# A third tile of quarter sums on GpSimd, and the last block's transposes in three groups

## The chip, the cores and the metric

The kernel runs on one core of a Trainium2 chip. The time is device microseconds of one execution; the number of a kernel is the median of its runs. Five engines run their own instruction queues, in order, and wait for each other on semaphores: PE (TensorE), DVE (VectorE), ACT (ScalarE), POOL (GpSimd) and SP (SyncE, which only issues DMAs here).

## The reference

One layer of a diffusion backbone over 1152 tokens of width 1024: 128 context tokens and 1024 latent ones. Two token mixers (a chunked bidirectional mLSTM and a pooling mixer) are merged and added to x; then comes the ConvFFN, at whose start the change lies:

```python
    y = jnp.einsum('bld,de->ble', jax.nn.sigmoid(ga) * ya + jax.nn.sigmoid(gb) * yb, w_out)
    x = x + gt1 * _rmsnorm(y, g_post_mix)
    h2 = _rmsnorm(x, g_pre_ffn) * (1 + sc2) + sh2
    up = _dwconv_rows(jnp.einsum('bld,df->blf', h2, w_up), conv_w, conv_b, grid)
    ug, uv = jnp.split(up, 2, axis=-1)
    f = jnp.einsum('blf,fd->bld', jax.nn.gelu(ug) * uv, w_down)
    x = x + gt2 * _rmsnorm(f, g_post_ffn)
```

`w_up` has 2 x 2816 columns: 22 blocks of 128 gate columns and 22 of value columns. The convolution has three taps along rows of 64 tokens.

## The kernel before

**Precision.** Every fp32 product is made of three passes over a high and a low part: x = hi + lo, and hi*hi, hi*lo, lo*hi are summed in PSUM. A split is two instructions: hi is a rounding copy (mostly ACT), lo is the difference (always DVE, recorded on L2375, the line of a helper).

**Tokens and features.** The 1152 tokens stand in three blocks b of 384, each of three tiles of 128. The normed input of the FFN, h2, is held with features on partitions: `H_hi` and `H_lo`, eight feature tiles k of 128 features by 1152 tokens. `w_out`'s product gives token tiles t = 0 to 8 with tokens on partitions, so h2 must be turned. Blocks 0 and 1 are turned through DRAM. The last block, b = 2, is turned by PE: `second_norm` (L1563) issues three transposes for a feature tile k into a PSUM bank, 6 or 7 in turn. From there `second_evac` on ACT (L2110, it calls `norm_evac`, L1802) writes scaled and shifted copies: `tsc2[k % 2]`, and for odd k `H_hi` too. On DVE `norm_split` (L2435) forms `H_hi` for even k and `H_lo` for all. `tsc2` has two slots, so the copy of turn k waits for the split of turn k - 2. `xt_free` counts evacuated turns, `h_split_done` the splits, 48 at the end of this stage.

**Where the turns stand.** PE's first products of the FFN are `first_up(half, b)` (L1698, half 0 gate and half 1 value), in the order (0,0), (0,1), (1,0), (1,1), (0,2), (1,2). Each is eight steps k of three matmuls with 384 columns (L1197 to L1199), into bank 3 * half + b. The table `LAST_TURNS` (L565) says behind which step a turn stands: turns 0 and 1 behind steps 6 and 7 of (1,0), turns 2 to 7 behind steps 0 to 5 of (1,1). (0,2) waits for the split of each k before its step k.

**Plain blocks.** The first three of the 22 feature blocks, f = 0, 1, 2, are done plainly: `plain_unit` on PE, and `plain_up(f, ...)` on ACT (L2180) and DVE (L2852). For each of three token blocks, first of the gate half and then of the value half, ACT writes the middle tap and the bias from PSUM (`conv_g`, `conv_v`, L2198), DVE adds the two outer taps (L2875, one input from PSUM), and for the gate ACT then applies gelu (L2203). `conv_gate_done` and `conv_value_done` count DVE's part. Weights come through a ring of three slots (`ring_hi` by ACT, `ring_lo` by DVE).

**Quarter sums.** The other 19 blocks are multiplied in a Strassen-like scheme, seven products instead of eight (`product(s, i, ...)`, L1591; its matmuls are on L1612). It needs sums of quarters of h2: `T1` to `T4`, each four feature tiles k by 576 tokens. `quarter_tiles(eng, done, k, before, lo, hi)` (L721) forms tile k of all four from `H_hi` and `H_lo`, in eight `tensor_tensor` instructions of 576 columns, lo to hi - 1 of them in one call; each waits for the one ahead of it. All are on L736. GpSimd does k = 0 and 1 (L1170), as soon as `h_split_done` is 48, and then `weight_sum(s, n)` for the weights (L1154). DVE does k = 2 and 3, in pieces that `between(f, block)` (L2973) puts behind the conv taps of a block (block is 0 to 2 for the gate half, 3 to 5 for the value half). `quarter_split(k)` rounds the four tiles on ACT (L2170, four instructions on L2177: `T_hi`) and takes the difference on DVE (L2845: `T_lo`). ACT's split of tile 2 stands ahead of `plain_up(2)`, its split of tile 3 between the halves of `plain_up(2)`.

**What the products wait for.** i = 0 and 1 use `H_hi` and `H_lo`; i = 0 waits for all nine gate blocks' taps (banks 0 and 1). i = 2 is the first that reads `T_hi` and `T_lo`: it waits for all four `quarter_lo`, the seventh value block's taps and its weight split:

```python
                if g == 0:
                    pe.wait_ge(conv_gate_done, NB * PLAIN)
                elif g == 2:
                    pe.wait_ge(conv_value_done, NB * (PLAIN - 1) + 1)
                pe.wait_ge(up_lo_done, g + 1)
                if s == 0:
                    pe.wait_ge(quarter_lo, KD // 2)
```

(`up_lo_done` is counted by `up_lo_split`, L2894; the last two lines stand in `up_pair`, ahead of i = 2.)

Of the kernel before, what the change touches and what calls it, by code (L numbers as in the profile page):

```python
# [30 lines left out]
KD = DM // P  # L31
# [4 lines left out]
NB = 3  # L36
# [72 lines left out]
def build(nc, x_prompt, x_sample, state_C, state_n, state_m, c, c_ctx, w_ada, b_ada, g_pre_mix, g_post_mix,  # L109
# [113 lines left out]
    def place(name, shape, dt=F32, at=None):  # L223
        size = int(np.prod(shape[1:])) * (2 if dt == BF16 else 4)
        off = base[0] if at is None else at
        if at is None:
            base[0] += (size + 31) // 32 * 32
        return nc.alloc_sbuf_tensor_at(name, shape, dt, offset=off)
# [117 lines left out]
    X1 = place("X1", [P, NT, DM], at=SC0 + 16 * T)  # L346
# [60 lines left out]
    ps = nc.alloc_psum_tensor("ps", [P, 8, 512], F32)  # L407
# [39 lines left out]
    xt_done, xt_free = S("xt_done"), S("xt_free")  # L447
# [38 lines left out]
    pool_sums, dve_sums = S("pool_sums"), S("dve_sums")  # L486
# [70 lines left out]
    def turned_block():  # L557

        return X1[:, 0:TB, :].rearrange("p t d -> p (t d)").rearrange("p (k s) -> p k s", s=BW)
# [2 lines left out]

        return z_turned[b].rearrange("(k p) s -> p k s", p=P)

    LAST_TURNS = {(1, 0): {6: 0, 7: 1}, (1, 1): {0: 2, 1: 3, 2: 4, 3: 5, 4: 6, 5: 7}}  # L565

    def out_bank(t):

# [152 lines left out]
    def quarter_tiles(eng, done, k, before, lo=0, hi=8):  # L721


        first, second = slice(0, HT), slice(HT, T)
        as_f32 = lambda ap: ap.bitcast(F32)
        x1, x2 = [[as_f32(h[:, k, c]) for h in (H_hi, H_lo)] for c in (first, second)]
        y1, y2 = [[as_f32(h[:, KD // 2 + k, c]) for h in (H_hi, H_lo)] for c in (first, second)]
        t1, t2, t3, t4 = [T_full[name][:, k, :] for name in quarters]
        steps = ((t1, x2[0], x2[1], ALU.add), (t2, y2[0], y2[1], ALU.add), (t3, t2, t1, ALU.subtract),
                 (t1, t1, x1[0], ALU.subtract), (t1, t1, x1[1], ALU.subtract), (t2, t2, t1, ALU.subtract),  # L730
                 (t4, y1[0], t2, ALU.subtract), (t4, t4, y1[1], ALU.add))
        for n, (out, a, b, op) in enumerate(steps):
            if lo <= n < hi:
                if n:
                    eng.wait_ge(done, before + n)
                eng.tensor_tensor(out, a, b, op).then_inc(done, 1)  # L736

    with nc.Block() as block:
# [288 lines left out]
        def _(pool):  # L1027
# [139 lines left out]
                pool.tensor_tensor(out, mid[f"g{half}"][:, :], mid[f"v{half}"][:, :], ALU.mult).then_inc(feature_done, 1)  # L1167

            pool.wait_ge(h_split_done, 2 * NB * KD)
            for k in range(2):  # L1170
                quarter_tiles(pool, pool_sums, k, 8 * k)
            for s in range(NP):
                weight_sum(s, 0)
# [15 lines left out]
        def _(pe):  # L1189
# [5 lines left out]
            def mm3(out, whi, wlo, xhi, xlo, first, last):  # L1195

                pe.matmul(out, whi, xhi, start=first, stop=False)  # L1197
                pe.matmul(out, whi, xlo, start=False, stop=False)  # L1198
                return pe.matmul(out, wlo, xhi, start=False, stop=last)  # L1199
# [36 lines left out]
            def norm_turn(Xt, out, b, k):  # L1236

                for j in range(TB):
                    mm = pe.transpose(out[:, j * P:(j + 1) * P], Xt[:, b * TB + j, k * P:(k + 1) * P], ident[:, :])
                return mm  # L1240
# [58 lines left out]
            for b in range(NB):  # L1299
# [5 lines left out]
                for k in range(KD):  # L1305
                    w = slice(k * P, (k + 1) * P)
# [213 lines left out]
            for d in range(KD):  # L1520
                s = S_YA + d
                pe.wait_ge(lo_ready, s + 1)
                for b in range(NB):
                    take0(3 * (U_YA + d) + b)
                    r = s % RS
                    for n, k in enumerate(HEAD_ORDER):
# [3 lines left out]
                        w = slice(k * P, (k + 1) * P)  # L1530
# [32 lines left out]
            def second_norm(b, k):  # L1563
                if k == 0:

                    pe.wait_ge(x_scaled, NT + TB * (b + 1))
                w = b * KD + k
                if k >= 2:
                    pe.wait_ge(xt_free, NB * KD + w - 1)
                norm_turn(X1, ps[:, 6 + w % 2, :], b, k).then_inc(xt_done, 1)  # L1570

            pe.wait_ge(evac1, 3 * KD)
            for t in range(NT):
# [124 lines left out]
            def first_up(half, b):  # L1698
                bank, done = ((0, done0), (3, done1))[half]
                r = (S_FF + half) % RS  # L1700
                if b == 0:
                    pe.wait_ge(lo_ready, S_FF + half + 1)

                    pe.wait_ge(evac2, NT) if half else pe.wait_ge(evac0, Q_FF)

                for k in range(KD):
                    if half == 0:
                        pe.wait_ge(h_split_done, KD * (NB + b) + k + 1)
                    w = slice(k * P, (k + 1) * P)
                    tok = slice(b * BW, (b + 1) * BW)  # L1710
                    mm = mm3(ps[:, bank + b, 0:BW], ring_hi[:, r, w], ring_lo[:, r, w], H_hi[:, k, tok],
                             H_lo[:, k, tok], k == 0, k == KD - 1)
                    if k in LAST_TURNS.get((half, b), ()):
                        second_norm(NB - 1, LAST_TURNS[half, b][k])
                mm.then_inc(done, 1)


# [17 lines left out]
        def _(act):  # L1735
# [66 lines left out]
            def norm_evac(src_of, ready, freed, coefA, sh, n0, tile, slots, b, ks=range(KD), direct=True):  # L1802

                for k in ks:
                    w = n0 + b * KD + k
                    ready(b * KD + k)
                    if w - n0 >= slots:

                        act.wait_ge(h_split_done, w - slots + 1)
                    parts = [(0, 0, P), (1, P, BW)] if b == 0 else [(1, 0, BW)]  # L1810
                    for cond, lo, hi in parts:
                        outs = [tile[:, w % slots, lo:hi]]
                        if direct and b and k % 2:

                            outs.append(H_hi[:, k, b * BW + lo:b * BW + hi])
                        for out in outs:
                            ins = act.activation(out, src_of(b * KD + k)[:, lo:hi], ACT.Identity,
                                                 scale=coefA[:, k, cond:cond + 1], bias=modT[:, sh + k, cond:cond + 1])
                    ins.then_inc(freed, 1)
# [253 lines left out]
            for d in range(KD):  # L2073
# [3 lines left out]
                k = HEAD_ORDER[d]  # L2077
                if k < HG:
                    w = load_of[("hm", k)]
                    act.wait_ge(tile_in[w % LS], 16 * (w // LS + 1))  # L2080
                else:
                    w = load_of[("o", k)]
# [27 lines left out]
            def second_evac(b, ks):  # L2110

                if b < NB - 1:
                    norm_evac(lambda w: turned_block()[:, w % KD, :], lambda w: act.wait_ge(turned_in, 48 if b else 16), xt_free,
                              coefA2, 24, 24, tsc2, 2, b, ks)
                else:
                    norm_evac(lambda w: ps[:, 6 + w % 2, :], lambda w: act.wait_ge(xt_done, NB * KD + w % KD + 1), xt_free,
                              coefA2, 24, 24, tsc2, 2, b, ks)

            for t in range(NT):
# [49 lines left out]

            def quarter_split(k):  # L2170

                if k >= 2:
                    act.wait_ge(dve_sums, 8 * (k - 1))
                else:
                    act.wait_ge(pool_sums, 8 * (k + 1))
                for name in ("T2", "T3", "T1", "T4"):
                    ins = act.activation(T_hi[name][:, k, :], T_full[name][:, k, :], ACT.Copy)  # L2177
                ins.then_inc(quarter_hi, 1)
# [186 lines left out]
        def _(dve):  # L2365
# [8 lines left out]
            def sub_hi(out, full, hi):  # L2374
                return dve.tensor_tensor(out, full, hi.bitcast(F32), ALU.subtract)  # L2375
# [394 lines left out]
            for d in range(KD):  # L2770
                if d == 4:
                    second_coef()
                k = HEAD_ORDER[d]
# [71 lines left out]
            def quarter_split(k):  # L2845

                dve.wait_ge(quarter_hi, k + 1)
                for name in quarters:
                    ins = sub_hi(T_lo[name][:, k, :], T_full[name][:, k, :], T_hi[name][:, k, :])
                ins.then_inc(quarter_lo, 1)  # L2850
# [122 lines left out]
            def between(f, block):  # L2973

                if (f, block) == (1, 1):
                    quarter_split(0)
                if (f, block) == (1, 2):
                    quarter_tiles(dve, dve_sums, 2, 0, 0, 3)
                if (f, block) == (1, 3):
                    quarter_tiles(dve, dve_sums, 2, 0, 3, 6)  # L2980
                if (f, block) == (1, 4):
                    quarter_tiles(dve, dve_sums, 2, 0, 6, 8)
                    quarter_tiles(dve, dve_sums, 3, 8, 0, 1)
                if (f, block) == (1, 5):
                    quarter_split(1)
                    next_weights(-1, 0)
                    next_weights(-1, 1)
                if (f, block) == (2, 0):
                    quarter_tiles(dve, dve_sums, 3, 8, 1, 5)
                if (f, block) == (2, 1):  # L2990
                    quarter_tiles(dve, dve_sums, 3, 8, 5, 8)
                if (f, block) == (2, 2):
                    quarter_split(2)
                if (f, block) == (2, 4):
                    quarter_split(3)
                    next_weights(-1, 2)

            plain_up(0, [[2], [3]])
# [159 lines left out]
```

## Time and profile before

| | |
|---|---|
| median of 3 runs | 1695.71 us (1695.4 to 1697.65) |
| the profiled execution, its own time | 1696.06 us |
| its span | 1694.2 us |
| mean granted clock of TensorE | 0.998 |
| busy: PE, DVE, ACT, POOL | 99%, 80%, 41%, 15% |

The span runs from the first to the last instruction. Busy time of PE is modelled from overlapping matmuls. Times in the views are microseconds from the start of the span. For reading them: a group such as "x4" is shown with the time from its first start to its last end, and an instruction that is held up by another engine after it has started shows that as a longer duration.

### The profile page before, as it was taken

The page shows a single profiled execution, that of the slowest core. Times are in us where ns is not written, and L with a number is a line of the kernel's source. Part 1 is how long each engine was busy: PE and PEld are TensorE (multiplying, and loading weights), DVE is VectorE, ACT ScalarE, POOL GpSimd, SP SyncE. Part 2 cuts the span into 40 slices and gives each one's busy share as a digit, 9 for nine tenths or more (in the row PEclk, how much of TensorE's full clock was granted, in tenths as well). Part 3 has the DMA queues.
Part 4 walks back from the last instruction along what each step waited for, and adds up shares of the span by engine and source line. Part 5 has one row for each costly group of instructions (what it writes and reads, how often), then busy time and mean ns, then how long its engine had stood idle before and what let it go on. Part 6 is the DMA issues. An engine that isn't in the chain of part 4 may idle for free.

```text
span 1694.2 us, 27385 instructions
## 1 busy us (share of the span) xinstructions
PE 1682.3 (99%) x10472; PEld 1602.8 (95%) x10472; DVE 1348.6 (80%) x2928; ACT 690.4 (41%) x1257; POOL 260.0 (15%) x260
## 2 busy tenths in 40 slices
PE   9999999999999999999999999999999999999998
PEld 4999999999999999999988999999999999888887
DVE  3789998899899887563655698888888788788998
ACT  4543222332333343641433644433434434444364
POOL 1010000000100100110010352444333333000000
PEclk9999999999999999999999999999999999999999
DMA  9314344464465653572367422323222221786876
GB/s 348 100 34 137 102 136 114 124 179 137 120 171 157 158 161 124 179 252 69 100 170 200 138 70 86 107 95 120 85 79 78 73 77 55 233 272 229 276 249 241
DMA packets 263494, 247.21 MB, mean 146 GB/s; under 512 B 55200, under 2 KB 207532, under 8 KB 263364
## 3 DMA queue, kind: packets, MB, share of 16 engines
q1 hardware_dynamic: 246516, 187.15, 37.3%
q0 software_dynamic: 11328, 40.36, 7.3%
q10 hardware_dynamic: 5520, 17.95, 2.7%
q8 instruction: 83, 1.36, 0.3%
q14 instruction: 47, 0.39, 0.1%
HBM read 186.99 MB, written 58.42 MB: 145 GB/s over the span
## 4 chain that ended last, share of the span: by engine, by line
PE 93%; DVE 3%; DMA 1%; SPq 1%; POOL 1%; ACT 1%; issue 0%; DVEq 0%; ACTq 0%
PE ps L1612 25%; PE ps L1197 12%; PE ps L1198 12%; PE ps L1199 12%; PE ps L1556 6%; PE ps L1630 5%; PE ps L1631 5%; PE ps L1629 5%; PE ps L1433 2%; PE ps L1435 2%; PE ps L1434 2%; DMA adaw<-in_w_ada_dram 1%; DVE T_full L736 1%; POOL T_full L736 1%; DVE T_lo L2375 1%; PE ps L1341 1%
## 5 line engine op out<-in xcount | busy, mean ns | idle before, releaser
L1197 PE MATMUL ps<-H_hi,ring_hi 128*128 128x384 f32 x1192 | 400.8, 336 | 0.1
L1199 PE MATMUL ps<-H_hi,ring_lo 128*128 128x384 f32 x1192 | 398.7, 334 | 0.0
L1198 PE MATMUL ps<-H_lo,ring_hi 128*128 128x384 f32 x1192 | 398.6, 334 | 0.0
L1197 PEld LDWEIGHTS ps<-H_hi,ring_hi 128*128 128x128 f32 x1192 | 223.9, 188 | 0.7 <-issue 0.6
L1198 PEld LDWEIGHTS ps<-H_lo,ring_hi 128*128 128x128 f32 x1192 | 223.9, 188 | 0.0
L1199 PEld LDWEIGHTS ps<-H_hi,ring_lo 128*128 128x128 f32 x1192 | 223.8, 188 | 0.0
L2375 DVE TENSOR_TENSOR up_lo<-up_raw,up_hi 128x512 fp32r<-128x512 f32 x114 | 88.4, 778 | 57.2 <-ACT up_hi L2168 57.2
L1612 PE MATMUL ps<-T_hi,up_hi 128*128 128x288 f32 x608 | 130.9, 297 | 2.1 <-DVE up_lo L2375 2.1
L1612 PE MATMUL ps<-T_hi,up_lo 128*128 128x288 f32 x608 | 131.0, 297 | 0.0
L1612 PE MATMUL ps<-T_lo,up_hi 128*128 128x288 f32 x608 | 130.7, 297 | 0.0
L2611 DVE SCALAR_TENSOR_TENSOR ada_part<-raw,condT,ada_part 128x128 f32<-128x128 f32 x448 | 120.4, 348 | 0.0
L1631 PE MATMUL ps<-B_hi,A_lo 128*128 128x512 f32 x308 | 119.9, 389 | 0.0
L1630 PE MATMUL ps<-B_lo,A_hi 128*128 128x512 f32 x308 | 119.9, 389 | 0.0
L1629 PE MATMUL ps<-B_hi,A_hi 128*128 128x512 f32 x308 | 119.9, 389 | 0.0
L1753 ACT ACTIVATE ring_hi<-raw 128x1024 fp32r<-128x1024 f32 (+1 forms) x61 | 60.9, 1000 | 128.5 <-DMA raw<-in_w_in_dram 61.8
L1612 PEld LDWEIGHTS ps<-T_hi,up_hi 128*128 128x128 f32 x608 | 98.6, 190 | 2.3 <-DVE T_lo L2375 2.3
L1612 PEld LDWEIGHTS ps<-T_hi,up_lo 128*128 128x128 f32 x608 | 98.7, 190 | 0.0
L1612 PEld LDWEIGHTS ps<-T_lo,up_hi 128*128 128x128 f32 x608 | 98.5, 190 | 0.0
L700 ACT ACTIVATE stage<-ps 128x384 f32<-128x384 f32 x72 | 35.1, 487 | 154.3 <-PE ps L1199 154.3
L1612 PE MATMUL ps<-H_hi,up_lo 128*128 128x288 f32 x456 | 97.9, 296 | 0.0
L1612 PE MATMUL ps<-H_hi,up_hi 128*128 128x288 f32 x456 | 97.8, 296 | 0.0
L2168 ACT ACTIVATE up_hi<-up_raw 128x512 fp32r<-128x512 f32 x114 | 68.9, 621 | 70.2 <-POOL up_raw L1154 70.0
(391 smaller groups left out, 3844.2 us busy)
## 6 DMA issues: line engine op xcount, KB each, us to landing
raw<-in_w_in_dram SPq DMA_DIRECT2D x44, 512.0 KB, 5.1
up_raw<-in_w_up_dram SPq DMA_DIRECT2D x38, 512.0 KB, 5.2
w_raw<-in_w_down_dram SPq DMA_DIRECT2D x66, 256.0 KB, 3.4
raw<-in_w_ada_dram SPq DMA_DIRECT2D x32, 512.0 KB, 5.5
X<-z_f SPq DMA_DIRECT2D x44, 256.0 KB, 3.9
GE<-z_gates SPq DMA_DIRECT2D x72, 128.0 KB, 4.0
w_sub<-in_w_down_dram SPq DMA_DIRECT2D x33, 256.0 KB, 3.9
adaw<-in_w_ada_dram SPq DMA_DIRECT2D x6, 1024.0 KB, 14.6
```

The source lines that it names most:

```text
L1197: pe.matmul(out, whi, xhi, start=first, stop=False)
L1198: pe.matmul(out, whi, xlo, start=False, stop=False)
L1199: return pe.matmul(out, wlo, xhi, start=False, stop=last)
L1556: mm = pe.matmul(ps[:, bank + hb, :], x[:, k, tok], w[:, hb * 512:(hb + 1) * 512], start=(n == 0 and first), stop=(n == KD - 1 and last))
L1612: mm = pe.matmul(ps[:, bank + sb, 0:SB], wt[:, w], x[:, k0 + k, cols], start=(k == 0 and n == 0), stop=(k == KD // 2 - 1 and n == 2))
L1629: pe.matmul(out, xhi, whi, start=first, stop=False)
L1630: pe.matmul(out, xhi, wlo, start=False, stop=False)
L1631: return pe.matmul(out, xlo, whi, start=False, stop=last)
L1753: act.activation(split_of(s)[0][:, 0:w], raw[:, n % RS, 0:w], ACT.Copy).then_inc(hi_ready, 2 if s == 1 else 1)
L2168: act.activation(up_hi[i][:, :], src, ACT.Copy).then_inc(up_hi_done, 1)
L2375: return dve.tensor_tensor(out, full, hi.bitcast(F32), ALU.subtract)
L2611: ins = dve.scalar_tensor_tensor(out=part, in0=w, scalar=condT[:, cond, k:k + 1], in1=part, op0=ALU.mult, op1=ALU.add)
```

## The change

Two parts. First, the turns of the last block: 0 to 3 stand together behind the last step of (1,0), 4 and 5 behind step 3 of (1,1), 6 and 7 behind step 1 of (0,2). They use banks 6, 7, 2, 5, 6, 7, 5, 6, so turn 4 waits for the evacuation of turn 0, 5 for 1, 6 for 3 and 7 for 4 (`TURN_AFTER`). (0,2) uses bank 2 and waits until turn 2 has been evacuated. Second, GpSimd forms the quarter sums of k = 2 too; DVE forms k = 3 alone, in four pairs of instructions, and its `T_lo` of k = 2 and 3 move one block earlier. The number of instructions of each kind is the same as before.

```diff
--- before.py
+++ after.py
@@ -562,7 +562,9 @@
 
         return z_turned[b].rearrange("(k p) s -> p k s", p=P)
 
-    LAST_TURNS = {(1, 0): {6: 0, 7: 1}, (1, 1): {0: 2, 1: 3, 2: 4, 3: 5, 4: 6, 5: 7}}
+    LAST_TURNS = {(1, 0): {7: (0, 1, 2, 3)}, (1, 1): {3: (4, 5)}, (0, 2): {1: (6, 7)}}
+    TURN_BANK = (6, 7, 2, 5, 6, 7, 5, 6)
+    TURN_AFTER = {4: 1, 5: 2, 6: 4, 7: 5}
 
     def out_bank(t):
 
@@ -1167,7 +1169,7 @@
                 pool.tensor_tensor(out, mid[f"g{half}"][:, :], mid[f"v{half}"][:, :], ALU.mult).then_inc(feature_done, 1)
 
             pool.wait_ge(h_split_done, 2 * NB * KD)
-            for k in range(2):
+            for k in range(3):
                 quarter_tiles(pool, pool_sums, k, 8 * k)
             for s in range(NP):
                 weight_sum(s, 0)
@@ -1564,10 +1566,9 @@
                 if k == 0:
 
                     pe.wait_ge(x_scaled, NT + TB * (b + 1))
-                w = b * KD + k
-                if k >= 2:
-                    pe.wait_ge(xt_free, NB * KD + w - 1)
-                norm_turn(X1, ps[:, 6 + w % 2, :], b, k).then_inc(xt_done, 1)
+                if k in TURN_AFTER:
+                    pe.wait_ge(xt_free, (NB + b) * KD + TURN_AFTER[k])
+                norm_turn(X1, ps[:, TURN_BANK[k], :], b, k).then_inc(xt_done, 1)
 
             pe.wait_ge(evac1, 3 * KD)
             for t in range(NT):
@@ -1703,6 +1704,8 @@
 
                     pe.wait_ge(evac2, NT) if half else pe.wait_ge(evac0, Q_FF)
 
+                if (half, b) == (0, NB - 1):
+                    pe.wait_ge(xt_free, (NB + b) * KD + 3)
                 for k in range(KD):
                     if half == 0:
                         pe.wait_ge(h_split_done, KD * (NB + b) + k + 1)
@@ -1711,7 +1714,8 @@
                     mm = mm3(ps[:, bank + b, 0:BW], ring_hi[:, r, w], ring_lo[:, r, w], H_hi[:, k, tok],
                              H_lo[:, k, tok], k == 0, k == KD - 1)
                     if k in LAST_TURNS.get((half, b), ()):
-                        second_norm(NB - 1, LAST_TURNS[half, b][k])
+                        for turn in LAST_TURNS[half, b][k]:
+                            second_norm(NB - 1, turn)
                 mm.then_inc(done, 1)
 
 
@@ -2113,7 +2117,7 @@
                     norm_evac(lambda w: turned_block()[:, w % KD, :], lambda w: act.wait_ge(turned_in, 48 if b else 16), xt_free,
                               coefA2, 24, 24, tsc2, 2, b, ks)
                 else:
-                    norm_evac(lambda w: ps[:, 6 + w % 2, :], lambda w: act.wait_ge(xt_done, NB * KD + w % KD + 1), xt_free,
+                    norm_evac(lambda w: ps[:, TURN_BANK[w % KD], :], lambda w: act.wait_ge(xt_done, NB * KD + w % KD + 1), xt_free,
                               coefA2, 24, 24, tsc2, 2, b, ks)
 
             for t in range(NT):
@@ -2169,8 +2173,8 @@
 
             def quarter_split(k):
 
-                if k >= 2:
-                    act.wait_ge(dve_sums, 8 * (k - 1))
+                if k == 3:
+                    act.wait_ge(dve_sums, 8)
                 else:
                     act.wait_ge(pool_sums, 8 * (k + 1))
                 for name in ("T2", "T3", "T1", "T4"):
@@ -2975,24 +2979,22 @@
                 if (f, block) == (1, 1):
                     quarter_split(0)
                 if (f, block) == (1, 2):
-                    quarter_tiles(dve, dve_sums, 2, 0, 0, 3)
+                    quarter_tiles(dve, dve_sums, 3, 0, 0, 2)
                 if (f, block) == (1, 3):
-                    quarter_tiles(dve, dve_sums, 2, 0, 3, 6)
+                    quarter_tiles(dve, dve_sums, 3, 0, 2, 4)
                 if (f, block) == (1, 4):
-                    quarter_tiles(dve, dve_sums, 2, 0, 6, 8)
-                    quarter_tiles(dve, dve_sums, 3, 8, 0, 1)
+                    quarter_tiles(dve, dve_sums, 3, 0, 4, 6)
                 if (f, block) == (1, 5):
                     quarter_split(1)
                     next_weights(-1, 0)
                     next_weights(-1, 1)
                 if (f, block) == (2, 0):
-                    quarter_tiles(dve, dve_sums, 3, 8, 1, 5)
+                    quarter_tiles(dve, dve_sums, 3, 0, 6, 8)
                 if (f, block) == (2, 1):
-                    quarter_tiles(dve, dve_sums, 3, 8, 5, 8)
-                if (f, block) == (2, 2):
                     quarter_split(2)
+                if (f, block) == (2, 3):
+                    quarter_split(3)
                 if (f, block) == (2, 4):
-                    quarter_split(3)
                     next_weights(-1, 2)
 
             plain_up(0, [[2], [3]])
```

## Rows read from the trace of the kernel before

**Rows 1.** Busy time of each engine, its share of the span, instructions.

```profile
PE 1682.3 (99%) x10472; PEld 1602.8 (95%) x10472; DVE 1348.6 (80%) x2928; ACT 690.4 (41%) x1257; POOL 260.0 (15%) x260
```

**Rows 2.** Waits of PE, 935 to 1060 us: total us, times, longest.

```profile
PE ps L1612 <- DVE up_lo L2375: 2.1, 1, 2.1
```

**Rows 3.** The chain that ended last: start us, us, what.

```profile
961.54 0.67 ACT H_hi L1817
962.24 0.57 DVE H_lo L2375
962.89 1.44 POOL T_full L736
...
1027.95 0.61 DVE up_lo L2375
```

**Rows 4.** Windows around the third L1612 product: PEclk is the granted clock.

```profile
1026.20:1030.00 3.80, 1.67 (x13) 1.47 (x12) 3.76 (x7) 1.66 (x4) 0.00 (x0) 1.00 0.00 0
1030.00:1033.50 3.50, 3.50 (x17) 3.50 (x17) 3.50 (x5) 0.00 (x0) 1.29 (x1) 0.51 0.46 181
```

**Rows 5.** PE's timeline, steps and turns of the last block: start us, us.

```profile
950.01 0.41 PE L1197 MATMUL ps<-H_hi,ring_hi 128*128 128x384 f32 x1
...
953.77 0.55 PE L1239 MATMUL ps<-ident,X 128*128 128x128 f32 x3
954.07 0.42 PE L1197 MATMUL ps<-H_hi,ring_hi 128*128 128x384 f32 x1
...
954.93 0.42 PE L1197 MATMUL ps<-H_hi,ring_hi 128*128 128x384 f32 x1
...
961.25 0.34 PE L1197 MATMUL ps<-H_hi,ring_hi 128*128 128x384 f32 x1
...
961.77 0.34 PE L1197 MATMUL ps<-H_hi,ring_hi 128*128 128x384 f32 x1
```

**Rows 6.** PE's timeline in the first stage, six transposes and what follows.

```profile
61.75 0.82 PE L1239 MATMUL ps<-ident,X 128*128 128x128 f32 x6
62.33 0.38 PE L1340 MATMUL ps<-vg_hi,H_hi 128*128 128x272 f32 x1
```

**Rows 7.** ACT's timeline; in brackets the idle time before, and its releaser.

```profile
954.36 0.67 ACT L1817 ACTIVATE tsc<-ps,modT,coefA 128x384 f32<-128x384 f32 x1 [1.63 <-PE ps L1239]
...
1003.36 2.41 ACT L2177 ACTIVATE T_hi<-T_full 128x576 fp32r<-128x576 f32 x4 [4.10 <-DVE T_full L736]
...
1019.61 2.40 ACT L2177 ACTIVATE T_hi<-T_full 128x576 fp32r<-128x576 f32 x4
```

**Rows 8.** DVE's timeline.

```profile
985.84 5.66 DVE L2375 TENSOR_TENSOR T_lo<-T_full,T_hi 128x576 fp32r<-128x576 f32 x4
...
998.17 1.74 DVE L736 TENSOR_TENSOR T_full<-T_full,H_lo 128x576 f32<-128x576 f32 x1
...
1008.95 1.51 DVE L2875 SCALAR_TENSOR_TENSOR conv_g<-ps,vT,conv_g 128x127 f32<-128x127 f32 x4
...
1019.06 2.75 DVE L2375 TENSOR_TENSOR T_lo<-T_full,T_hi 128x576 fp32r<-128x576 f32 x4
1022.59 2.68 DVE L2875 SCALAR_TENSOR_TENSOR conv_v<-ps,vT,conv_v 128x127 f32<-128x127 f32 x6 [0.78 <-ACT conv_v L2198]
```

**Rows 9.** The quarter sums by engine: durations min/median/max ns, first, last.

```profile
L736 POOL TENSOR_TENSOR T_full<-T_full x4: 1424/1432/1434, 966.8 to 985.0; 128x576 f32<-128x576 f32 x4
...
L736 DVE TENSOR_TENSOR T_full<-T_full x4: 749/758/758, 994.2 to 1015.6; 128x576 f32<-128x576 f32 x4
```

**Rows 10.** POOL's timeline: its last quarter sum, its second weight sum.

```profile
988.39 1.83 POOL L736 TENSOR_TENSOR T_full<-T_full,H_lo 128x576 f32<-128x576 f32 x1
...
997.56 1.73 POOL L1154 TENSOR_TENSOR up_raw<-up_raw 128x512 f32<-128x512 f32 x1
```

**Rows 11.** PE's timeline, the first and the third L1612 product.

```profile
1020.01 0.43 PE L1612 MATMUL ps<-H_hi,up_hi 128*128 128x288 f32 x2
...
1028.69 0.51 PE L1612 MATMUL ps<-T_hi,up_hi 128*128 128x288 f32 x2 [2.13 <-DVE up_lo L2375]
```

## The prediction

> **What bounds the kernel now.** The page first: PE is busy 99% of the span [rows 1], so nothing shortens the kernel but a wait of PE's, and over the span these are few. The view of waits, for PE from 935 to 1060 us, shows a single one of size: 2.1 us before a product of the feature halves (L1612), ended by DVE's up_lo [rows 2]. The chain of waits tells where it begins. It leaves PE at the last block's turns, goes through ACT and DVE to 962.8 us, through GpSimd's quarter sums from 962.89 on, and then through ACT and DVE to up_lo at 1028.6, after which PE runs on [rows 3]. So from 954 to 1029 us PE isn't the bound. The bound is the chain turns, splits, quarter sums, conv taps, T_lo, up_lo, and PE, which runs ahead of it, waits at its end.
>
> That wait costs twice. In the 3.8 us around it PE is busy for 1.67, and in the 3.5 us behind it the granted clock is 0.51, of full 2.4 GHz at 1.2, before it is 1.00 again [rows 4]. These 3.5 us at half clock lose (1 - 0.51) x 3.5 = 1.7 us. What the change can win here at most is therefore 2.1 + 1.7 us, and what PE saves at the turns.
>
> **The turns.** A step of three matmuls with no turn behind it takes 961.77 - 961.25 = 0.52 us, one with a turn 954.93 - 954.07 = 0.86, so a turn costs PE 0.34 [rows 5]. Does a group cost less? In the first stage six transposes stand together, and the next matmul begins 62.33 - 61.75 = 0.58 us after the first of them [rows 6]; two turns of 0.34 are 0.68, and the matmul behind a transpose is up to 0.1 late. So twelve transposes cost about four turns: I take 8 x 0.34 in both kernels. What PE saves is its waits between the turns. The first product of (1, 0) starts at 950.01 and (0, 2) at 961.77 [rows 5]; with sixteen steps and six turns and no wait it would start at 950.01 + 16 x 0.52 + 6 x 0.34 = 960.4, or 960.5 with a first step that is 0.1 longer. The last two turns, 0.7 us, then stand in (0, 2) itself, so PE is 0.6 us earlier at its end. Since PE runs ahead of the chain, that alone is worth nothing.
>
> The price is the chain's start. Turns 6 and 7 now come behind step 1 of (0, 2): 960.5 + 2 x 0.52 = 961.5. ACT sees a turn 954.36 - 953.77 = 0.6 us after its first transpose [rows 5, 7], so tsc of turn 6 starts at 962.1, and tsc and H_hi of turn 7 follow, each about 0.57 behind the last (0.67 long, a tenth of it overlapped), H_hi at 963.2. In the kernel before that H_hi starts at 961.54 [rows 3]: **+1.7 us** for the splits, for the quarter sums that wait for all 48 of them, and for every ring split behind. The first four turns don't make up for it, as turn 0 comes 0.5 us later than before too. The added wait for turn 2's bank in front of (0, 2) costs nothing: its evacuation is over by 957.5.
>
> **The quarter sums.** Tile 2's eight sums leave DVE. They take 0.76 us each and one of them 1.74 [rows 8, 9]: **-7.0 us**. But the sums of tile 3 and other work of DVE now run while GpSimd sums tile 2, and the two engines are in each other's way. A GpSimd sum takes 1.43, but 1.83 with DVE's T_lo beside it; the four T_lo of tile 0 take 5.66 us beside GpSimd and 2.75 alone, 2.9 more for some three meetings; a DVE sum that starts inside a GpSimd weight sum (997.56, 1.73 long) takes 1.74 for 0.76 [rows 8 to 10]. It looks as if the one waits until the other's instruction ends. I take 1.1 us for a meeting. (By the Trainium skill, GPSIMD Engine Reference, Key points, GpSimd shares its SBUF interfaces with VectorE and contends with instructions there that have two SBUF inputs or run in a 2-port mode. By this rule the conv taps, which read PSUM, stay as they are, and sums and splits pay, as in the trace. Its table of Engine selection says to keep elementwise work on VectorE as GpSimd is about twice slower; 1.43 against 0.75 agrees.)
>
> How many meetings are new? GpSimd's second tile ends at 988.39 + 1.83 = 990.2, the third begins 1.7 later and takes 8 x 1.5 plus 0.4 for each meeting, to some 1006.5, and two weight sums follow to 1010. DVE's two-input work in 992 to 1010 is the fourth T_lo of tile 0, ring_lo 5 and tile 3's first six sums, in pairs behind three blocks' taps. Of these eight I count six: a pair's first often falls in a gap. **+6.6 us.** ACT's work doesn't grow.
>
> **The order on DVE.** ACT does T_hi of tile 3 between the last gelu and the first conv_v of f = 2, 2.40 us from 1019.61, and DVE can't start conv_v's taps before 1022.59. In the kernel before DVE fills this gap with T_lo of tile 2, from 1019.06 for 2.75, and idles for 0.78 [rows 7, 8]. The change moves this T_lo ahead of the last gate block's taps, where it delays them, the gelu and T_hi, and leaves 1022.59 - 1019.1 = 3.5 us of idle time on DVE: **+2.7 us**. T_lo of tile 3, one block earlier than before, still ends before the same up_lo.
>
> **Sum.** up_lo, and PE's third product: +1.7 - 7.0 + 6.6 + 2.7 = +4.0 us, from 1028.7 to 1032.7 [rows 11]. A new wait of PE stands ahead of it: the first product needs the last gate block's taps, which ended at 1019.1 and now end at 1019.1 + 1.7 - 7.0 + 6.6 + 2.75 = 1023.1, while PE is there at 1020.0 - 0.6 [rows 8, 11]. The two products from 1020.01 to 1026.56 (1028.69 less 2.13) then take till 1029.7, or 1031.4 if the half clock falls on them: hidden before 1032.7. PE's second gap is thus 1.3 to 3 us instead of 2.1. Whether the clock falls again behind it, I can't read; if it doesn't, 1.7 us come back. I take half, -0.8: **+3.2 us**. The profiled execution took 1696.06, 1.9 more than its span and 0.35 more than the median of the runs, 1695.71; on that median the sum gives 1698.9.
>
> **Bounds.** If no meeting is new, 6.6 us go, and the path is PE's: third product at 1026.56 - 0.6 = 1025.9, -2.8, without a gap and so without half clock, -1.7: 1691.2. If each meeting costs a whole GpSimd instruction, 1.43, it is +2.0 and no clock comes back: +6.0, 1701.7. The turns' delay between 0 and 1.9, the gap on DVE between 2.0 and 2.75.
>
> **Rivals.**
> - Faster: sums on DVE and GpSimd hardly meet, or meet without cost, so that taking eight sums from DVE wins. For it: most of GpSimd's first tile ran at 1.43 beside DVE's taps. Against it: [rows 8, 10]. It decides below about 2.5 us for all new meetings. 1691.2.
> - Nothing measurable: the turns' delay is absorbed by the idle time that ACT and DVE have before 980 us, or fewer meetings, 3 of 6: +3.2 less 1.7 to 3.3, about 1697. Against it: the chain has no slack there.
> - GpSimd becomes the bound: ACT must wait for its third tile before the first conv_g of f = 2. Before, ACT waited 4.10 us for DVE's tile and began T_hi at 1003.36, and DVE came to those taps at 1008.95 [rows 7, 8], about 2.6 us after conv_g was written. Now T_hi begins at 1006.6, and DVE is there at about 1014 (1008.95 + 1.7 - 7.0 + 6.6, and five sums of tile 3, 3.8, that stood behind): some 4 us of margin. If GpSimd is later than that, each further us adds one: 1702 and more.
> - The change does nothing at the turns: grouping saves no time in PE. I hold this anyway; it is in the sum.
>
> **How the numbers follow.** The forecast has 0.60, faster 0.15, nothing measurable 0.17, GpSimd's bound 0.08. A measurement tells 0.2%, 3.4 us, from no change. The forecast of +3.2 lies beside this bound, with the clock's 0.8 to either side; I give 0.34 of its 0.60 to slower, 0.23 to the same and 0.03 to faster. Together: faster 0.18, the same 0.39, slower 0.43. The forecast's own range is 1696.5 to 1701.7; the range is 1692.3 to 1701.8, which leaves out the far end of the faster case and GpSimd's.
>
> **What would show it.** POOL's first T_full at 964.5 and not 962.9; turns 6 and 7 behind L1197's second step of (0, 2), and ACT's tsc after them; DVE's sums and T_lo near 1.8 where they meet GpSimd; a wait of PE of 3 to 4 us before the first L1612, ended by DVE's conv_g; DVE idle for 3.5 us until conv_v; the third product at 1032.7. I am wrong if PE enters L1612 without a wait, or if DVE's sums of tile 3 are all 0.76.

## The result, and the profile after

The kernel is slower: 1700.14 us, median of 14 runs (1699.14 to 1701.33), against 1695.64 for the kernel before on the same chip, also 14 runs. The ratio is 1.0026, with a 95% interval of 1.0019 to 1.0033: 3.2 to 5.6 us more. The profiled execution has a span of 1698.5 us. Line numbers of the changed kernel are up to four higher (L1612 is L1613, L2375 is L2379).

PE's line of the page hardly changes, and its waits, for the same stretch as in [rows 2], do:

```profile
PE 1684.3 (99%) x10472; PEld 1604.2 (94%) x10472; DVE 1348.8 (79%) x2920; ACT 690.1 (41%) x1257; POOL 276.0 (16%) x268
...
PE ps L1613 <- DVE conv_g L2879: 3.9, 1, 3.9
PE ps L1613 <- DVE up_lo L2379: 0.5, 1, 0.5
```

One wait of 2.1 us has become two, 4.4 in all, and the longer one stands ahead of the first product. The timeline of PE shows the groups of turns and both products:

```profile
953.72 1.47 PE L1241 MATMUL ps<-ident,X 128*128 128x128 f32 x12
954.95 0.42 PE L1199 MATMUL ps<-H_hi,ring_hi 128*128 128x384 f32 x1
...
960.94 0.81 PE L1241 MATMUL ps<-ident,X 128*128 128x128 f32 x6
...
1022.91 0.85 PE L1613 MATMUL ps<-H_hi,up_hi 128*128 128x288 f32 x2 [3.94 <-DVE conv_g L2879]
...
1032.40 0.50 PE L1613 MATMUL ps<-T_hi,up_hi 128*128 128x288 f32 x2 [0.46 <-DVE up_lo L2379]
```

The third product starts 3.7 us later than in [rows 11]. The windows around both products (span of time, sum, busy us and count of PE, PEld, DVE, ACT, POOL, then granted clock, DMA share, GB/s), to set against [rows 4], show half clock behind the first gap now, and none behind the third product:

```profile
1019.30:1023.00 3.70, 0.09 (x1) 0.09 (x1) 3.52 (x6) 0.95 (x3) 0.00 (x0) 0.79 0.00 0
1023.00:1027.00 4.00, 4.00 (x17) 4.00 (x18) 0.70 (x2) 4.00 (x8) 0.00 (x0) 0.50 0.37 150
...
1030.00:1033.50 3.50, 3.04 (x23) 2.83 (x22) 3.43 (x7) 1.68 (x3) 0.00 (x0) 1.00 0.00 0
...
1034.00:1038.00 4.00, 4.00 (x32) 4.00 (x31) 4.00 (x6) 0.00 (x0) 1.61 (x1) 1.00 0.55 193
```

At half clock the first two products take from 1022.91 to 1031.94 (1032.40 less 0.46), 9.0 us, where they took 6.55 before. That stretch hides almost whole in the wait for up_lo.

DVE's timeline, against [rows 8]:

```profile
986.89 6.89 DVE L2379 TENSOR_TENSOR T_lo<-T_full,T_hi 128x576 fp32r<-128x576 f32 x4
...
994.86 2.73 DVE L738 TENSOR_TENSOR T_full<-H_hi,H_lo 128x576 f32<-128x576 f32 x2
997.51 2.45 DVE L2379 TENSOR_TENSOR ring_lo<-raw,ring_hi 128x1024 fp32r<-128x1024 f32 x1
...
1002.09 1.87 DVE L738 TENSOR_TENSOR T_full<-T_full,H_hi 128x576 f32<-128x576 f32 x1
...
1005.90 1.87 DVE L738 TENSOR_TENSOR T_full<-T_full 128x576 f32<-128x576 f32 x1
...
1008.86 3.85 DVE L2379 TENSOR_TENSOR T_lo<-T_full,T_hi 128x576 fp32r<-128x576 f32 x4
...
1026.30 1.51 DVE L2879 SCALAR_TENSOR_TENSOR conv_v<-ps,vT,conv_v 128x127 f32<-128x127 f32 x4 [3.44 <-ACT conv_v L2202]
```

Four T_lo take 6.89 and 3.85 us where two groups at the same places took 5.66 and 2.75, sums take 1.87 where one alone takes 0.75, and DVE idles 3.44 us ahead of conv_v's taps, not 0.78. GpSimd's timeline beside it:

```profile
963.94 3.80 POOL L738 TENSOR_TENSOR T_full<-H_hi,H_lo 128x576 f32<-128x576 f32 x2 [11.63 <-DVE H_lo L2379]
...
997.05 1.83 POOL L738 TENSOR_TENSOR T_full<-T_full,H_hi 128x576 f32<-128x576 f32 x1
998.96 2.29 POOL L738 TENSOR_TENSOR T_full<-T_full,H_lo 128x576 f32<-128x576 f32 x1
...
1001.33 2.01 POOL L738 TENSOR_TENSOR T_full<-T_full 128x576 f32<-128x576 f32 x1
...
1005.33 1.82 POOL L738 TENSOR_TENSOR T_full<-T_full,H_lo 128x576 f32<-128x576 f32 x1
```

Read the two together. The DVE sum of 1002.09 ends at 1003.96, and the GpSimd sum that ran beside it at 1001.33 + 2.01 = 1003.34. The one of 1005.90 ends at 1007.77, its neighbour at 1007.15. ring_lo ends at 999.96, its neighbour at 998.88. Each DVE instruction ends 0.62 us (ring_lo 1.08, it has 1024 columns) behind the end of GpSimd's, whatever was left of that when it started: it stands still until GpSimd's instruction is over. It goes the other way too. GpSimd's next sum starts while DVE's is still on, and ends 1.29 us behind the end of that: at 1001.25 behind ring_lo's 999.96, at 1005.25 behind the sum's 1003.96. So when both have such work, they take turns.

### The profile page after: what moved, and what is told of

It reads as the page before. It is cut to its first block, busy times and chain, and to the rows that moved or that the text cites. A ratio compares the mean times of both kernels' runs of the same rounds, so it can differ in the third digit from the quotient of the medians.

```text
span 1698.5 us, 27386 instructions
## 1 busy us (share of the span) xinstructions
PE 1684.3 (99%) x10472; PEld 1604.2 (94%) x10472; DVE 1348.8 (79%) x2920; ACT 690.1 (41%) x1257; POOL 276.0 (16%) x268
## 4 chain that ended last, share of the span: by engine, by line
PE 84%; DVE 8%; DMA 3%; ACT 1%; POOL 1%; SPq 1%; issue 1%; DVEq 0%; ACTq 0%; POOLq 0%
PE ps L1613 18%; PE ps L1199 12%; PE ps L1200 12%; PE ps L1201 12%; PE ps L1558 6%; PE ps L1630 4%; PE ps L1632 4%; PE ps L1631 4%; PE ps L1435 2%; PE ps L1437 2%; PE ps L1436 2%; DVE mid_g L2929 1%; DVE up_lo L2379 1%; DMA w_sub<-z_w_diff 1%; DVE T_lo L2379 1%
## 5 line engine op out<-in xcount | busy, mean ns | idle before, releaser
L2379 DVE TENSOR_TENSOR up_lo<-up_raw,up_hi 128x512 fp32r<-128x512 f32 x114 | 89.7, 789 | 57.2 <-ACT up_hi L2172 57.2
L1613 PE MATMUL ps<-T_hi,up_hi 128*128 128x288 f32 x608 | 130.6, 296 | 1.0 <-ACT held_g L2214 0.6
L1613 PE MATMUL ps<-T_lo,up_hi 128*128 128x288 f32 x608 | 130.2, 296 | 0.0
L1613 PE MATMUL ps<-T_hi,up_lo 128*128 128x288 f32 x608 | 130.2, 296 | 0.0
L1613 PE MATMUL ps<-H_hi,up_hi 128*128 128x288 f32 x456 | 99.0, 299 | 3.9 <-DVE conv_g L2879 3.9
L1613 PEld LDWEIGHTS ps<-T_hi,up_hi 128*128 128x128 f32 x608 | 97.9, 189 | 1.9 <-ACT held_g L2214 1.1
L1613 PE MATMUL ps<-H_hi,up_lo 128*128 128x288 f32 x456 | 98.6, 298 | 0.0
L1613 PE MATMUL ps<-H_lo,up_hi 128*128 128x288 f32 x456 | 98.4, 298 | 0.0
L1613 PEld LDWEIGHTS ps<-T_hi,up_lo 128*128 128x128 f32 x608 | 98.0, 189 | 0.0
L1613 PEld LDWEIGHTS ps<-T_lo,up_hi 128*128 128x128 f32 x608 | 98.0, 189 | 0.0
```

Of the source, the lines that this page charges most:

```text
L1613: mm = pe.matmul(ps[:, bank + sb, 0:SB], wt[:, w], x[:, k0 + k, cols], start=(k == 0 and n == 0), stop=(k == KD // 2 - 1 and n == 2))
```

## The experiments

All differences below are against runs of the kernel before on the same chip, and their 95% intervals reach some 1.5 us to either side; what is finer than that is read from the traces, one of each kernel. The stages ahead of the FFN end up to 0.7 us apart from execution to execution, so times within a trace are counted from the first product of f = 0, at 941.38 us in the kernel before, 941.21 in the changed one, and between 941.00 and 941.70 in the others.

| kernel | time against before, us | first product of f = 0 to first T_full on POOL | first T_full to third product | first product of f = 0 to down stage |
|---|---|---|---|---|
| before | 0 | 21.51 | 65.80 | 507.72 |
| changed | +4.5 | 22.73 | 68.46 | 511.55 |
| turns_only | +1.5 | 22.73 | 65.78 | 508.90 |
| sums_only | +3.3 | 21.14 | 68.47 | 510.03 |
| splits_back | +3.1 | 22.73 | 67.04 | 509.32 |
| no_third_tile | -2.1 | 22.91 | 62.55 | 505.67 |
| filled_gap | +0.4 | 21.21 | 65.82 | 507.71 |
| reordered | -3.9 | 21.21 | 63.54 | 503.57 |
| reordered_turns | -2.9 | 22.73 | 62.63 | 504.66 |

**turns_only and sums_only: the change in two halves.** The first has the new `LAST_TURNS`, `TURN_BANK` and `TURN_AFTER` alone, the second all but these.

```diff
-    LAST_TURNS = {(1, 0): {6: 0, 7: 1}, (1, 1): {0: 2, 1: 3, 2: 4, 3: 5, 4: 6, 5: 7}}
+    LAST_TURNS = {(1, 0): {7: (0, 1, 2, 3)}, (1, 1): {3: (4, 5)}, (0, 2): {1: (6, 7)}}
+    TURN_BANK = (6, 7, 2, 5, 6, 7, 5, 6)
```

> The kernel before with the changed turns alone (groups of four, two and two, their banks and waits); the quarter sums as before. Theory (the chain from the last turn to up_lo has no slack): POOL's first T_full starts about 1 us later than in the kernel before (962.89), the third product about 1.7 later than 1028.69 less the shift of the origin, so near 1030.0, and the time is 1.2 to 1.7 above the kernel before, ratio 1.0007 to 1.0010. Rival 1 (the later turns are absorbed by idle time of ACT and DVE before 980 us): third product within 0.4 of 1028.7, time within 0.4. Rival 2 (what PE saves at the turns counts): 0.5 below.

> The kernel before with GpSimd's third quarter tile and the order on DVE and ACT that goes with it; turns as before. Theory (meetings of DVE and GpSimd at 1.1 us each, and the gap that ACT's T_hi of tile 3 leaves on DVE): third product near 1031.0 (+2.3), first product waits near 3 us for DVE's conv_g, time 2.3 to 3 above the kernel before, ratio 1.0014 to 1.0018, and this one's and turns_only's differences add up to the whole change's 4.5. Rival (meetings are free and the turns are all of the loss): at or below the kernel before, down to 1691.

Measured: turns_only 1697.56 us against 1696.04, ratio 1.0011 (1.0003 to 1.002); sums_only 1699.31, 1.0020 (1.0012 to 1.0029). Together 4.8, for 4.5 of the whole. At the start of the down stage the traces have +1.2 and +2.3; the profiled execution of sums_only has its remaining microsecond in the down stage, which takes 240.7 us there and 239.2 before, and why is open. Up to the third product the table parts the halves cleanly. The turns move the start of the quarter sums and nothing behind it (65.78 for 65.80). The sums leave the start alone and stretch what follows by 2.7. PE's saving at the turns is no gain anywhere: in turns_only PE waits longer, twice, for the same DVE results.

```profile
1020.35 0.53 PE L1613 MATMUL ps<-H_hi,up_hi 128*128 128x288 f32 x2 [1.26 <-DVE conv_g L2879]
...
1029.84 0.50 PE L1613 MATMUL ps<-T_hi,up_hi 128*128 128x288 f32 x2 [2.85 <-DVE up_lo L2379]
```

**splits_back: only the order on DVE undone.**

```diff
-                if (f, block) == (2, 1):
+                if (f, block) == (2, 2):
                     quarter_split(2)
-                if (f, block) == (2, 3):
+                if (f, block) == (2, 4):
                     quarter_split(3)
```

> The changed kernel with T_lo of tile 2 back behind the last gate taps of f = 2 and T_lo of tile 3 back behind the fifth block, as in the kernel before. Theory (moving T_lo ahead of the last gate taps cost 2.7 us, as DVE then stands idle while ACT does T_hi of tile 3): DVE's idle time ahead of conv_v near 1026 falls from 3.44 to under 1 us, the third product comes 2.7 earlier than 1032.40, near 1029.7, and the time falls from 1700.1 to about 1697.4. Rival (the end is set elsewhere, by GpSimd's third tile or by PE): the time stays within 0.7 of 1700.1.

Measured: 1699.17 us, 1.0019 (1.001 to 1.0028), 3.1 above the kernel before, where the changed kernel is 4.5 above it; in the trace the third product comes 1.4 us earlier, not 2.7. (The down stage comes 2.2 earlier; where the 0.8 between comes from is open.) The timelines, two lines of ACT and then DVE, show where the other 1.3 stay:

```profile
1019.56 0.52 ACT L2207 ACTIVATE conv_g<-conv_g 128x384 f32<-128x384 f32 x1 [2.60 <-DVE conv_g L2879]
1019.99 0.65 ACT L2202 ACTIVATE conv_g<-ps,vT 128x384 f32<-128x384 f32 x1
...
1020.68 1.26 DVE L2879 SCALAR_TENSOR_TENSOR conv_g<-ps,vT,conv_g 128x378 f32<-128x378 f32 x2 [1.15 <-ACT conv_g L2202]
1021.85 2.76 DVE L2379 TENSOR_TENSOR T_lo<-T_full,T_hi 128x576 fp32r<-128x576 f32 x4
1025.38 2.67 DVE L2879 SCALAR_TENSOR_TENSOR conv_v<-ps,vT,conv_v 128x127 f32<-128x127 f32 x6 [0.77 <-ACT conv_v L2202]
```

The gap ahead of conv_v closes, as expected (0.77). But a new one of 1.15 us opens ahead of the third gate block's taps: ACT can only start conv_g there (1019.99) after its gelu of the block before (1019.56), and with tile 2's sums gone nothing stands on DVE meanwhile; in the kernel before three sums of tile 3 stood there, 2.3 us. In the changed kernel T_lo of tile 2 fills that gap and leaves the other.

**no_third_tile: the same instructions on DVE and ACT, no third tile on GpSimd.** The splits of tile 2 read a tile of `H_hi`, so this kernel leaves out the sums of tile 2.

```diff
-            for k in range(3):
+            for k in range(2):
                 quarter_tiles(pool, pool_sums, k, 8 * k)
...
+                    src = H_hi[:, 2, 0:HT].bitcast(F32) if k == 2 else T_full[name][:, k, :]
-                    ins = act.activation(T_hi[name][:, k, :], T_full[name][:, k, :], ACT.Copy)
+                    ins = act.activation(T_hi[name][:, k, :], src, ACT.Copy)
```

> The changed kernel, with GpSimd's third quarter tile left out: the splits of tile 2 read a tile of H_hi in place of the sums, so that all of ACT's and DVE's instructions stay. Theory (six meetings at 1.1 us come from the third tile): DVE's T_full and T_lo from 992 to 1011 us fall to 0.75 each, the DVE chain is some 6.6 us shorter, PE is held by its own work, the third product at 1026 to 1027 and the time 1.5 to 3 below the kernel before, near 1693. Rival (long T_full and T_lo come from something else than GpSimd's instructions beside them): third product near 1032, time near 1700.

Measured: 1693.96 us, 0.9989 (0.998 to 0.9998). DVE's timeline, for the instructions shown above of the changed kernel:

```profile
987.19 5.64 DVE L2380 TENSOR_TENSOR T_lo<-T_full,T_hi 128x576 fp32r<-128x576 f32 x4
...
993.91 1.54 DVE L738 TENSOR_TENSOR T_full<-H_hi,H_lo 128x576 f32<-128x576 f32 x2
995.54 1.23 DVE L2380 TENSOR_TENSOR ring_lo<-raw,ring_hi 128x1024 fp32r<-128x1024 f32 x1
...
998.88 1.74 DVE L738 TENSOR_TENSOR T_full<-T_full,H_hi 128x576 f32<-128x576 f32 x1
...
1002.49 0.76 DVE L738 TENSOR_TENSOR T_full<-T_full 128x576 f32<-128x576 f32 x1
...
1004.33 2.76 DVE L2380 TENSOR_TENSOR T_lo<-T_full,T_hi 128x576 fp32r<-128x576 f32 x4
```

The third tile costs 1.25 us at the first T_lo group, 1.19 at the pair of sums, 1.22 at ring_lo, 1.11 at the sum of 1002.49, 1.09 at the second T_lo group and 0.2 at two others together: 6.1 us. From POOL's first sum to the taps of conv_v it is 56.46 us here (964.23 to 1020.69) and 62.36 in the changed kernel, 5.9 less. The sum of 998.88 takes 1.74 here too: it meets a weight sum (L1156), as the one of 998.17 did in [rows 8]. That meeting went over to another sum when tile 2's left DVE. The third product comes as much earlier, 5.9 (62.55 for 68.46). PE's own pace does not hold it, as the expectation had it: PE still waits 1.1 us for up_lo there.

**filled_gap: the kernel before, without its half clock.**

```diff
                 if s == 0:
+                    for _ in range(14):
+                        pe.matmul(ps[:, SLOT_BANK[2], 0:SB], H_hi[:, 0, 0:P], H_hi[:, 0, 0:SB], start=True, stop=True)
                     pe.wait_ge(quarter_lo, KD // 2)
```

> The kernel before, with 14 matmuls of 128x288 more in PE's gap ahead of the third product; their results are overwritten. They take some 1.9 us of the 2.1 us wait, so that PE is not idle there. Theory (through the up stage the chain over DVE sets the pace, not PE; runs so far show 420.2 to 420.4 us from the third product to the down stage whether the half clock falls behind that product or ahead of it): the granted clock behind the third product is 1.00 or the dip is shorter, the seventh product of the first pair starts up to 1.5 us earlier than 14.4 us behind the third, and the time does not change, within 0.4 of the kernel before. Rival (PE sets the pace, and the dip costs 1.7 us): the time falls by 1.3 to 1.7 us, ratio 0.9990 to 0.9992.

Measured: 1696.42 us against 1696.01, ratio 1.0001 (0.9993 to 1.001). The windows of [rows 4]:

```profile
1026.20:1030.00 3.80, 3.52 (x27) 3.32 (x27) 3.77 (x7) 1.15 (x3) 0.00 (x0) 1.00 0.00 0
1030.00:1033.50 3.50, 3.50 (x28) 3.50 (x28) 3.50 (x5) 0.00 (x0) 1.30 (x1) 1.00 0.55 207
```

The clock stays at 1.00, and the seventh product of the first pair starts at 1041.03, 12.9 us behind the third and not 14.4. But the down stage starts 507.71 us behind the first product of f = 0, for 507.72: the 1.5 us are gone. The loss can be followed from pair to pair. Counted from the first product of f = 0, the third product of the second pair comes 1.8 us earlier than in the kernel before (1.5 of the clock, 0.3 of a pause ahead of (1, 0) that only the trace of the kernel before has), that of the ninth at the same time (267.92 and 267.93). The reason is the pace of the two engines: in the kernel before, PE's third products of the second to the ninth pair follow each other every 22.4 us (1052.65 to 1209.31, seven pairs), but DVE's last held_g sums of a pair every 23.2 us from 1069.72 to 1185.97 (five pairs), and every 22.2 from 1208.13 on. A PE that is ahead comes to wait for DVE's results before that. PE now waits where it did not before: twice for ACT's held_g, 0.4 and 0.3 us, at 1169.68 and 1192.90, and up to 0.2 at several products around them. held_g in turn comes when DVE is done with the taps before it, at the same time in both kernels. The timelines of ACT, first of filled_gap, then of the kernel before:

```profile
1168.98 0.65 ACT L2212 ACTIVATE held_g<-ps 128x576 f32<-128x576 f32 x1 [3.49 <-DVE mid_g L2927]
```

```profile
1168.94 0.65 ACT L2210 ACTIVATE held_g<-ps 128x576 f32<-128x576 f32 x1 [3.47 <-DVE mid_g L2925]
```

**reordered and reordered_turns: another order, with the old division.** The kernel before, two tiles on GpSimd and two on DVE, with DVE's items behind its blocks of taps in this order (a block's number counts gate 0 to 2, value 3 to 5), and on ACT T_hi of tile 1 ahead of its last conv_v of f = 1.

```diff
+                if (f, block) == (0, 2):
+                    quarter_tiles(dve, dve_sums, 2, 0, 0, 1)
+                if (f, block) == (0, 4):
+                    quarter_tiles(dve, dve_sums, 2, 0, 1, 2)
+                if (f, block) == (1, 0):
+                    quarter_tiles(dve, dve_sums, 2, 0, 2, 3)
                 if (f, block) == (1, 1):
-                    quarter_split(0)
+                    quarter_tiles(dve, dve_sums, 2, 0, 3, 5)
                 if (f, block) == (1, 2):
-                    quarter_tiles(dve, dve_sums, 2, 0, 0, 3)
+                    quarter_split(0)
...
                 if (f, block) == (2, 2):
+                    quarter_tiles(dve, dve_sums, 3, 8, 7, 8)
+                    next_weights(-1, 1)
                     quarter_split(2)
-                if (f, block) == (2, 4):
                     quarter_split(3)
```

> The kernel before, its division of the sums (two tiles each) and its turns kept, but with DVE's work in another order: the first five sums of tile 2 one by one in the gaps in which DVE waits for ACT, from the end of f = 0 on; T_lo of tile 0 one block later, when GpSimd's second tile has ended; ACT's T_hi of tile 1 ahead of its last conv_v of f = 1; T_lo of tiles 2 and 3 both behind the last gate taps; up_lo 1 and 2 later. Theory (what counts is how often DVE's two-input work meets GpSimd's and how long DVE waits for ACT): T_lo of tile 0 takes about 2.8 us instead of 5.66, the DVE chain ends 3 to 4 us earlier, the third product comes at PE's own pace, 26.4 to 27.2 us behind 1000 for 1028.7 before, with a wait under 0.7 us, and the time is 1.5 to 2.3 below the kernel before. Rival (early sums only move the meetings, and delay the ring splits): third product within 0.5 of 1028.7, time the same.

> The same order on DVE and ACT, with the changed turns in groups. Theory (the turns delay the chain's start by 1.2 and save PE 0.6): where the chain now has slack at its end, the delay is partly hidden; third product between 0.6 earlier and 0.9 later than with the turns one by one, time within 0.7 of that run. Rival (the chain is still the bound everywhere): 1.2 to 1.5 later, as in the kernel with the turns alone.

Measured: reordered 1692.13 us against 1696.01, ratio 0.9977 (0.9968 to 0.9987), faster than both kernels; reordered_turns 1693.15, 0.9985 (0.9976 to 0.9994), 1.0 behind it. With the turns in groups the third product comes 0.6 us later (85.36 for 84.76 from the first product of f = 0), as expected, and the down stage 1.1; the time lies between the expected 0.7 and the rival's 1.2. In reordered PE has no wait in 935 to 1260 us. DVE's timeline:

```profile
990.77 2.83 DVE L2376 TENSOR_TENSOR T_lo<-T_full,T_hi 128x576 fp32r<-128x576 f32 x4
...
1013.88 6.54 DVE L2376 TENSOR_TENSOR T_lo<-T_full,T_hi 128x576 fp32r<-128x576 f32 x8
1020.34 3.83 DVE L2876 SCALAR_TENSOR_TENSOR conv_v<-ps,vT,conv_v 128x127 f32<-128x127 f32 x8
1024.09 1.28 DVE L2376 TENSOR_TENSOR up_lo<-up_raw,up_hi 128x512 fp32r<-128x512 f32 x2
...
1029.40 1.60 DVE L2912 TENSOR_TENSOR held_g<-held_g,ps 128x576 f32<-128x576 f32 x2
```

T_lo of tile 0 takes 2.83 us instead of 5.66, and eight T_lo stand in the gap that ACT's T_hi of tile 3 leaves, so that DVE goes on without an idle moment to its first held_g sums. Its first held_g sum starts 67.1 us behind POOL's first T_full, and 71.4 in the kernel before (1034.33): the chain is 4.3 us shorter. The third product gains 2.6 us, counted from the first product of f = 0, as PE has no wait left there. The down stage starts 4.15 earlier, and the other 1.6 are the half clock: without a wait the granted clock is 1.00 in each of five windows from 1018 to 1038 us, and the seventh product comes 12.8 us behind the third, not 14.4. Here the gain stays, since DVE is 4.6 us earlier than in the kernel before and PE never waits for it. The expectation of 1.5 to 2.3 left the clock out. These are several moves at once; how the gain on DVE divides among them no run shows.

## Why the prediction was right

The forecast was +3.2 us and 1698.9; measured were +4.5 and 1700.14, inside the range, by the mechanism that was forecast. That the sum met the third product within 0.1 us is in part luck: the terms are off by up to 0.9, and their errors cancel. The 1.3 us by which the change missed (+4.5 for +3.2) are the clock's term, 0.8, and some 0.5 in the down stage. (The chances do not add up to the last digit either: 0.17 + 0.23 is 0.40 and 0.34 + 0.08 is 0.42, where 0.39 and 0.43 stand.)

**The turns, +1.7.** POOL's first T_full came at 963.94, 22.73 behind the first product of f = 0, for 21.51 before and 21.1 to 21.2 in the three other kernels with turns one by one. Before's own trace has a pause of 0.3 us ahead of (1, 0) that these lack. So the turns cost 1.2 against that trace and 1.5 to 1.6 otherwise; turns_only measured +1.5 us. All of it reached the end. PE's own saving is the forecast 0.6: it is ready for the first product of the quarter scheme at 77.76, and at 78.36 in filled_gap. It was worth nothing, as written.

**DVE's sums, -7.0.** Mis-sized by 0.9. I took off the 1.74 of one of the eight sums, but its meeting with the weight sum stayed and only fell on another sum: 8 x 0.76 is 6.1.

**Six meetings, +6.6.** The five of size cost 1.1 to 1.25 each and two small ones 0.2: 6.1 us, by no_third_tile. The price of 1.1 held, the count was one too many.

**The order on DVE, +2.7.** The idle time came out as predicted (3.44). Putting the order back gives 1.4 only, as 1.15 us stay as the wait for ACT's gelu ahead of the third gate block, which now has nothing on DVE to hide it. I had not seen that wait: it comes from taking the sums away, not from the place of T_lo. The two are 2.6 together, for the +2.7.

**Their total.** -6.1 + 6.1 + 2.7 is +2.7 for the sums, where my terms gave +2.3; the traces show 68.46 - 65.80 = 2.66. With the turns it is 3.9 us at the third product (91.19 against 87.31 from the first product of f = 0), and the sum said +4.0. The first product's wait was predicted as 3 to 4 us, ended by conv_g, and is 3.94. The second gap was predicted as 1.3 to 3 us and is 0.46: the half clock cost the two products ahead of it 2.5 us (9.0 for 6.55), not 1.7. DVE's whole busy time, 1348.6 us before and 1348.8 after, says the same as the two equal terms.

**The clock, -0.8.** This term is wrong; it should be nothing. The half clock did stay away behind the third product (it fell behind the first), so PE ran the pair 1.5 us faster, but filled_gap shows that the kernel gains nothing by that. The changed kernel's own trace has it too: against the kernel before its third product is 3.9 us late in the first pair, 2.4 in the second and 3.8 from the ninth on. Through the first pairs of the up stage, to 1193 us, DVE sets the pace, and a PE that is ahead waits for it. [Rows 3] end where PE runs on, and I let the chain of DVE end there too. Without the term the forecast is 1699.7 on the median of 1695.71; the changed kernel measured 4.5 above the kernel before, +4.0 by that sum. The half microsecond left over lies in the down stage, which takes between 239.2 and 240.7 us (first to last matmul) in these traces with no order that follows the edits; its cause is open.

**The rivals.** Meetings that cost nothing: refuted by no_third_tile, which is what that case would have been, and it is faster than the kernel before. Slack ahead of 980 us: none, by turns_only. GpSimd the bound: ACT began conv_g at 1009.50 and DVE came to its taps at 1013.84, with conv_g written at 1010.15: 3.7 us of margin, for the 4 I had read. Grouping does save PE time, 0.6 us, but no run shows it at the end.

## What to carry to other kernels

Moving work from a busy engine to an idle one is worth what it takes off, less one meeting for each two-input instruction that the other engine now runs beside; here eight sums of 0.76 us were bought with 6.1 us of such meetings, and nothing was won. Look first for an order: of two kernels with the same instructions on each engine, the one whose T_lo stands behind GpSimd's last sum and whose long item fills DVE's wait for ACT is 3.9 us faster, 1.6 of them as PE's clock no longer falls. And when PE's wait disappears, ask whether the engine that it waited for is still late in the next stage before counting PE's gain.

## What the runs showed that was not expected

A half clock can be free, and it is so only while another engine is behind. Fourteen matmuls in a gap of 2.1 us kept the granted clock at 1.00 where it had been 0.51 for 3.5 us, and the time moved by +0.4 us within an interval of -1.2 to +1.7. In reordered, where DVE is 4.6 us earlier, the same full clock gives 1.6 us in the trace, and they stay.

A meeting costs what is left of the other's instruction. DVE's ends a fixed 0.62 us behind GpSimd's: the sum of 1005.04, beside a GpSimd sum that is over at 1005.25, takes 0.82, and the one of 1005.90, beside one that has 1.25 us to go, takes 1.87. GpSimd pays in return: about 0.4 us beside 576 columns (1.83 for 1.43), 0.86 beside ring_lo's 1024 (2.29). The taps, which read PSUM and one tile of SBUF, kept their times: four of 128x127 take 1.50 from 999.89 on, beside GpSimd's sum of 998.96 to 1001.25, and 1.51 from 1026.30 on, where GpSimd is idle. The Trainium skill (GPSIMD Engine Reference, Key points) says that GpSimd contends with VectorE instructions that have two SBUF inputs or run in a 2-port mode. The traces agree for two inputs, at 1.09 to 1.25 us a meeting, and show no stall of the taps; the length of the stall is the traces' own, and no run here is about the 2-port mode.
